# Loading keys and queries of an attention head in three groups, and the last wait on another engine

## What is computed

```python
def diff_attend(q, k, v, lam, mask):
    s = jnp.einsum('bqhmd,bkhmd->bhmqk', q, k).astype(F32) * (D_DH ** -0.5)
    if mask is not None:
        s = jnp.where(mask[None, None, None], s, -jnp.inf)
    p = jax.nn.softmax(s, axis=-1)
    a = p[:, :, 0] - lam * p[:, :, 1]
    return jnp.einsum('bhqk,bkhv->bhqv', a, v.astype(F32))
```

## Time and profile before

| | us |
|---|---|
| median of 3 runs | 1052.09 |
| lowest and highest | 1050.88, 1052.38 |
| the profiled execution | 1057.25 |
| its span, first to last instruction | 1055.4 |

### The profile page before, as it was taken

The page is one execution under the profiler, slowest core; times in us unless marked ns, Lnnn a source line. Parts: engine busy times, 40 slices in busy tenths (PEclk is TensorE's granted clock), DMA queues, the critical chain, the costliest instruction groups (busy, mean ns, idle before and its releaser), DMA issues.

```text
span 1055.4 us, 12423 instructions
## 1 busy us (share of the span) xinstructions
PE 1012.0 (96%) x4780; PEld 832.6 (79%) x4780; DVE 677.4 (64%) x990; ACT 529.0 (50%) x726; POOL 146.7 (14%) x181
## 2 busy tenths in 40 slices
PE   4999999999999999999999999998999999999996
PEld 3788888888777888788778888887778888888784
DVE  5677775226555664345246655687699898888882
ACT  4433322446454554333353223364587877868772
POOL 1000011111202121211112000011211211212112
PEclk9999999999999999999999999998899999999998
DMA  9238856262615334424347434227799999999994
GB/s 304 67 143 305 306 216 221 94 247 86 215 41 210 112 143 140 141 110 160 125 160 262 157 125 160 101 102 270 303 425 381 405 384 404 396 392 405 383 368 63
DMA packets 62180, 238.20 MB, mean 226 GB/s; under 512 B 5392, under 2 KB 5568, under 8 KB 49792
## 3 DMA queue, kind: packets, MB, share of 16 engines
q1 hardware_dynamic: 41152, 163.32, 40.5%
q0 software_dynamic: 20960, 73.99, 21.1%
HBM read 199.92 MB, written 48.15 MB: 235 GB/s over the span
## 4 chain that ended last, share of the span: by engine, by line
PE 62%; issue 25%; DMA 5%; POOL 3%; DVE 3%; ACT 1%; SPq 0%; POOLq 0%; ACTq 0%; DVEq 0%
PE ps L469 15%; PE ps L471 15%; PE ps L470 15%; PE ps L1792 3%; PE ps L1793 3%; PE ps L1811 2%; DMA q_tok<-z_q 2%; PE ps L1768 2%; PE ps L1848 1%; POOL x_exp L800 1%; POOL out_y L811 1%; DMA rows_a<-x_slots 1%; DMA x_tok<-in_x_prompt 1%; PE ps L1941 1%; PE ps L1957 1%
## 5 line engine op out<-in xcount | busy, mean ns | idle before, releaser
L469 PE MATMUL ps<-w_hi,s_hi 128*128 128x512 f32 x672 | 268.1, 399 | 1.4 <-ACT stage L930 1.1
L471 PE MATMUL ps<-w_lo,s_hi 128*128 128x512 f32 x672 | 263.4, 392 | 0.0
L470 PE MATMUL ps<-w_hi,s_lo 128*128 128x512 f32 x672 | 263.2, 392 | 0.0
L469 PEld LDWEIGHTS ps<-w_hi,s_hi 128*128 128x128 f32 x672 | 127.4, 190 | 27.5 <-DVE s_hi L1255 1.4
L471 PEld LDWEIGHTS ps<-w_lo,s_hi 128*128 128x128 f32 x672 | 126.9, 189 | 26.9
L470 PEld LDWEIGHTS ps<-w_hi,s_lo 128*128 128x128 f32 x672 | 127.2, 189 | 25.5 <-issue 0.2
L930 ACT ACTIVATE stage<-ps,x_rstd 128x512 f32<-128x512 f32 x64 | 43.9, 688 | 188.3 <-PE ps L471 188.3
L405 DVE TENSOR_TENSOR w_lo<-raw,w_hi 128x2048 fp32r<-128x2048 f32 x42 | 96.2, 2290 | 44.6 <-ACT w_hi L400 44.4
L400 ACT CAST w_hi<-raw 128x2048 fp32r<-128x2048 f32 x42 | 80.0, 1909 | 15.3 <-DMA raw<-in_w_in 10.0
L441 DVE TENSOR_TENSOR lo_x<-raw_x,w_hi 128x2048 fp32r<-128x2048 f32 x32 | 72.1, 2287 | 10.8 <-ACT w_hi L418 10.8
L441 DVE TENSOR_TENSOR lo_x<-raw_x,hi_x 128x2048 fp32r<-128x2048 f32 x32 | 72.2, 2287 | 8.6 <-ACT hi_x L418 8.5
(11 more groups left out here) (306 smaller groups left out, 1859.2 us busy)
## 6 DMA issues: line engine op xcount, KB each, us to landing
raw<-in_w_in SPq DMA_DIRECT2D x32, 1024.0 KB, 7.3
raw_x<-in_w_up SPq DMA_DIRECT2D x30, 1024.0 KB, 20.4
raw_x<-in_w_down SPq DMA_DIRECT2D x18, 1024.0 KB, 20.8
raw<-in_w_gate SPq DMA_DIRECT2D x16, 1024.0 KB, 19.2
raw_x<-in_w_gate SPq DMA_DIRECT2D x16, 1024.0 KB, 19.8
raw<-in_w_down SPq DMA_DIRECT2D x14, 1024.0 KB, 21.6
x_slots<-in_c_empty SPq DMA_DIRECT2D x4, 2112.0 KB, 16.4
x_exp<-x_slots POOLq DMA_DIRECT2D x16, 528.0 KB, 13.0
```

Source lines behind the costliest of these rows:

```text
L469: nc.tensor.matmul(out, s_h, w_h, start=first, stop=False)
L470: nc.tensor.matmul(out, s_l, w_h, start=False, stop=False)
L471: return nc.tensor.matmul(out, s_h, w_l, start=False, stop=last)
```

## The change

The loads of a head are cut into four functions. The prompt's keys of head h + 2 are loaded in the iteration of tile 3, after a wait for group 3 of head h + 1; the cached keys and the prompt's queries in that of tile 4, after a wait for group 5; the sample's keys and queries after that, behind the wait for group 6 as before. The queries, one DMA before, are two now. The sample's rows count on a semaphore of their own, kq_rest_in, for which TensorE waits ahead of group 6; ahead of group 0 it waits for 48 per head instead of 64. The waits for the last scatters are removed from the end of GpSimd's program, and stand at the end of SyncE's. GpSimd's waits between further passes stay.

```diff
-    kq_in, lam_loaded = sem("kq_in"), sem("lam_loaded")
+    kq_in, kq_rest_in, lam_loaded = sem("kq_in"), sem("kq_rest_in"), sem("lam_loaded")
...
         with sp.If(passes > 1):
             with sp.Fori(1, passes) as j:
                 expert_pass(j)
+        sp.wait_ge(y_half_landed, 16)
+        for k in range(2):
+            sp.wait_ge(y_scattered[k], 16 * (NE // 2))
...
+        def load_prompt_keys(h):
+            dma(k_tok[:, 0:PT, :], tiles(z["k"], h * DV, (h + 1) * DV, 0, PT)).then_inc(kq_in, 16)
+
+        def load_cached_keys(h):
+            dma(kc_tok[:, :, :], a["cache_k"][0, 0, :, h, :].rearrange("(t p) c -> p t c", p=P)).then_inc(kq_in, 16)
+
+        def load_prompt_queries(h):
+            dma(q_tok[:, 0:PT, :], tiles(z["q"], h * DV, (h + 1) * DV, 0, PT)).then_inc(kq_in, 16)
+
+        def load_sample_keys(h):
+            lo, up = h * DV, (h + 1) * DV
+            dma(k_tok[0:SAMPLE, PT, :], z["k"][PROMPT:REAL, lo:up]).then_inc(kq_rest_in, 16)
+            dma(q_tok[:, PT, :], z["q"][PROMPT:ROWS, lo:up]).then_inc(kq_rest_in, 16)
+
         def load_keys(h):
-            lo, up = h * DV, (h + 1) * DV
-            dma(k_tok[:, 0:PT, :], tiles(z["k"], lo, up, 0, PT)).then_inc(kq_in, 16)
-            dma(k_tok[0:SAMPLE, PT, :], z["k"][PROMPT:REAL, lo:up]).then_inc(kq_in, 16)
-            dma(kc_tok[:, :, :], a["cache_k"][0, 0, :, h, :].rearrange("(t p) c -> p t c", p=P)).then_inc(kq_in, 16)
-            dma(q_tok[:, :, :], tiles(z["q"], lo, up)).then_inc(kq_in, 16)
+            load_prompt_keys(h)
+            load_cached_keys(h)
+            load_prompt_queries(h)
+            load_sample_keys(h)
...
             if g < UNITS:
+                if t == 3 and h + 2 < H:
+                    pool.wait_ge(tr_evacuated, small_n["head", h + 1, 3] + 1)
+                    load_prompt_keys(h + 2)
                 if t == PT and h + 2 < H:
+                    pool.wait_ge(tr_evacuated, small_n["head", h + 1, 5] + 1)
+                    load_cached_keys(h + 2)
+                    load_prompt_queries(h + 2)
                     pool.wait_ge(tr_evacuated, small_n["head", h + 1, HEAD_USES - 1] + 1)
-                    load_keys(h + 2)
+                    load_sample_keys(h + 2)
...
                     expert_pass(j)
                     all_landed(j)
-        all_landed(0)
...
         def head_part(h, k):
             if k == 0:
-                pe.wait_ge(kq_in, 64 * (h + 1))
+                pe.wait_ge(kq_in, 48 * (h + 1))
+            if k == HEAD_USES - 1:
+                pe.wait_ge(kq_rest_in, 32 * (h + 1))
```

## The result

The changed kernel takes 1047.31 us in the median of 13 runs (1046.02 to 1049.05), the kernel before 1052.09 in 13 runs beside it (1049.84 to 1057.29). The ratio is 0.9947, with a 95% interval of 0.9933 to 0.9961: 5.6 us faster, between 4.1 and 7.0. The two medians by themselves lie 4.8 us apart. Forecast were 1043.7 us, 8.4 us faster, in a range of 1040.5 to 1047.6; the measured median lies only 0.3 us inside the slow end of that range.

What follows compares the result with a forecast made beforehand. TensorE, busy 96% of the span, was taken to bound the kernel. Gains of 7.7 us (loads) and 0.7 us (last wait) sum to 8.4 us, from 1052.09 to 1043.7 us, range 1040.5 to 1047.6.

Steps and rivals of the forecast that it cites:

- TensorE's two waits: Key transposes at two heads wait for the queries' load, 2.50 and 2.02 us; both waits were to go whole.
- The price of a stall: Excess of two head periods over 42.76 us: 4.02 and 3.65, together 7.67 us, 4.52 idle and 3.15 low clock.
- part two: End of program, last wait on SyncE: 0.7 us gain (0.2 to 1.4), GpSimd's drain starting some 3.5 us behind its branch.
- half of part one: Rival, heads: only part of the stalls can be won, 3.8 + 0.7 us, 1047.6 us; chance 0.10.
- part one: Heads, loads issued by groups: both stalls and their low clock go, 7.7 us gain (7.3 to 8.0; idle time alone 4.5).
- The new waits of GpSimd: Tiles 3 and 4: the awaited groups are already copied, at 249.67 and 259.91, so the waits cost nothing.
- The sample rows: Heads: they still wait until 269.84, but TensorE needs them only three units of some 8 us behind the first group.
- The landing of 10.9 us: Heads: longest landing allowed for the prompt queries, from 263.8 to 274.7, 5.6 us before TensorE needs them.
- The store of tile 4: GpSimd, heads: issued at about 271.0 instead of 272.8, with two load issues ahead of it instead of four.
- The rival of the hidden drain: End of program: GpSimd's drain hides whole behind the landing, 7.7 + 3.6 = 11.3 us gain, 1040.8 us; chance 0.15.
- The drain bound to the landing: Rival, end of program: GpSimd's drain needs the scatters landed, so moving the wait gives 0, 1044.4 us; chance 0.10.
- The slower case: Rival, expert stage: five more stops with low clock, 2.5 us each, outweigh the gain, 1056.2 us; chance 0.05.

Runs made afterwards that it cites:

- the traced pair: First profiled executions of the kernel before and of the changed kernel, no further edit: 1057.25 us and 1048.92 us; also called the first pair.
- the wait alone: Kernel before with only the wait for the last scatters moved from GpSimd to the end of SyncE's program, loads unchanged: ratio 0.9989.
- the second trace: Kernel before, no edit, run against itself and profiled again: ratio 1.0005, profiled execution 1052.70 us.
- late loads: Kernel before with the loads of head h + 2 and their wait moved behind the store of tile 4: ratio 1.0044.
- the first trace: Kernel before, no edit, the profiled execution that the prediction was read from: 1057.25 us.
- the third: Kernel before, no edit, one further profiled execution: 1052.59 us.
- the fourth: Kernel before, no edit, one further profiled execution: 1053.72 us.
- queries last: Changed kernel with the prompt queries loaded behind the wait for group 6, prompt and cached keys still early: ratio against the kernel before 0.9945.

## Why the prediction was right, and where its size was off

- That TensorE's two waits go whole, and the low clock with them: right. The periods of 42.61 and 42.66 even lie 0.10 to 0.15 us below the first head's, which I had taken as the base, so the gain in the traced pair was 7.9 us and not 7.67.
- The price of a stall: this is the term that was mis-sized. I read 4.02 and 3.65 us from one execution, with low clock in both, and took the differences of that execution over to the median of the plain runs. Five traces with the old loads give 7.9, 3.1, 5.5, 6.2 and 3.8 us for the two heads (sums of the excess in the table, the wait alone as the fifth), mean 5.3. With 1.2 for part two that is 6.5 us, 1045.6 us from 1052.09. The two measured ratios give 5.6 and 7.6. So the mechanism held and the size did not: that 1047.31 still lies in the range is owed to its slow end of 1047.6, which comes from the rival of half of part one and not from the sum.
- The sign was there. The profiled execution stood 5.16 us above the median of its kernel. Its mean clock of 0.985, below that of all 35 runs of the kernel before in the series of the second trace (0.986 to 0.993), is a weaker sign: among those runs clock and time don't go together (the fastest, 1050.45 us, has 0.988, the slowest, 1056.23, 0.990), and the trace of late loads has 0.989 with two falls in the heads. I made half of part one a rival at 0.10, with 1047.6 us; it came nearest to the measured 1047.31. But the mean of the traces, 5.3 us, lies between its 3.8 and my 7.7, and so does what the two measurements leave for part one.
- The new waits of GpSimd cost nothing at tile 3 and at the first wait of tile 4, as said. The sample rows were in time. The landing of 10.9 us that I allowed for was twice too long: the prompt queries landed in 5.4 and 5.5 us, 11 us ahead of TensorE and not 5.6.
- The store of tile 4 was issued at 273.6, not at 271.0: its data came only then, behind a wait of 1.72 us for ScalarE. Nothing waited for it.
- Part two, a branch of some 3.5 us ahead of the drain: 3.05 us in the changed kernel, so 1.1 us in the first pair, 1.2 by the means, instead of 0.7, inside the ends of 0.2 to 1.4. The rival of the hidden drain (3.6 us) falls with the drain at 1043.1. The drain bound to the landing fails as I had priced it, with no gain: the span ended 1.2 us earlier behind the last scatter's issue. As a mechanism it was half right, since three of six drains ended 2.06 us behind the landing.
- On the two rules of the Trainium skill: the delay behind a taken branch ("Runtime: NRT & Kernel Launch", "Instruction fetch mechanics") agrees in kind with the 3.05 us between GpSimd's branch and its drain, where nothing else is waited for; no run shows that a fetch fills this time. That boilerplate drains take about 12 ns on all engines ("VectorE: DVE Perf Modes", "The DRAIN you can't avoid") fits SyncE here (7 to 13 ns where it had just waited), but not VectorE (57), ScalarE (81) or GpSimd (3587 to 7037 ns). The page speaks of drains that the runtime adds; these carry a line of the kernel, the end of its block, so they may not be the ones it means, and the prediction should not have put its figure on them.
- The slower case did not come: between 750 us and TensorE's last matmuls no trace has more than one stretch at the lower clock, which is what the first had.

What stays open: why GpSimd's drain takes 3.6 us with nothing under way, and what it does in the 2.06 us behind a landing; why the clock falls behind one short stop and not behind its like; and a wait of TensorE for rows_a, around 735 us. It is there or not between traces of the same kernel (1.1 us in the first two of before, none in the third and the fourth; 1.7 with the wait alone, none in the changed kernel, 1.8 with queries last), so it is no part of the change.

## What to carry to other kernels

A stall in a trace is one draw. Where its end is a DMA's landing and the low clock of TensorE follows it in some executions only, the price jumps between them (1.4 to 4.3 us here for the same stall), and a forecast for the median has to come from several traces. A transfer that is late by 2 us behind a burst need not be issued 8 us earlier: it was enough to take the other 1.1 MB out from ahead of it, which also let it leave 2.0 us earlier, or to issue the whole burst 6 us earlier. A wait at the end of a program belongs on an engine whose drain is short, but the gain is bounded by what the other engine does behind its own branch, and by what its drain still needs behind the landing.

## What the runs showed of the hardware

- TensorE's clock fell from its upper to its lower level (granted clock 1.00 to 0.50) behind each of six stalls of 1.98 to 2.95 us in the heads, and behind none of six of 1.25 to 1.83 us. A stall with a fall cost 1.7 to 1.8 us beyond its idle time, one without 0.15 to 0.21. In the expert stage it fell at 1003 in the first trace behind a stop of 0.94 us, and did not in the second behind one of 0.90.
- GpSimd's drain took 3.587 us behind landed scatters (seven traces), 3.656 to 3.917 when entered some 4.1 us behind the issue of the last one (five), and 7.037 when entered just ahead of that issue (one). In three of these last six it ended 2.06 us behind the landing of the last scatter.
- From GpSimd's branch past unexecuted code to its drain it took 3.05 us in the changed kernel and 3.05 in the kernel with the wait alone, and 2.9 to 3.0 in the three other traces with the wait on SyncE.
- The same load of 640 KB, behind the same 1.1 MB, landed in 9.6 to 10.9 us in four traces of one kernel, and TensorE's idle time went with it, from 1.25 to 2.50 us.
